# A mixture-of-experts stage with experts ranked by token count, and with fewer slots for the small ones

## What is computed

```python
def swiglu(h, w1, w3, w2):
    return (jax.nn.silu(h @ w1) * (h @ w3)) @ w2

def moe_swiglu(h, router_w, router_b, w1, w3, w2):
    logits = (h @ router_w).astype(jnp.float32) + router_b.astype(jnp.float32)
    top_logit, top_idx = lax.top_k(logits, TOP_K)
    top_p = jax.nn.softmax(top_logit, axis=-1)
    gates = jnp.einsum('btk,btke->bte', top_p,
                       jax.nn.one_hot(top_idx, N_EXPERTS, dtype=jnp.float32)).astype(h.dtype)
    y = jnp.zeros_like(h)
    for e in range(N_EXPERTS):
        y = y + gates[..., e:e + 1] * swiglu(h, w1[e], w3[e], w2[e])
    return y
```

## Time and profile before

| | us |
|---|---|
| median of 3 runs | 3539.58 |
| lowest and highest run | 3536.91, 3546.32 |
| the profiled execution, whole | 3545.75 |
| its span in the profile | 3543.9 |
| the expert work of the eight experts, first matmul to the last | 1724.9 to 2294.2 |
| PE busy over the span | 3007.5 (85%) |

### The profile page before, as it was taken

How to read it: one execution, slowest core, us unless ns; L and a number is a source line. 1 busy time by engine, 2 the same in 40 slices (tenths; PEclk the granted TensorE clock), 3 DMA queues, 4 the chain that set the end, 5 groups by cost and what they waited for, 6 DMA issues and landing times. The chain is left out here.

```text
span 3543.9 us, 59895 instructions
## 1 busy us (share of the span) xinstructions
PE 3007.5 (85%) x26727; PEld 2046.0 (58%) x26727; DVE 1130.1 (32%) x1816; ACT 548.0 (15%) x994; POOL 214.4 (6%) x200
## 2 busy tenths in 40 slices
PE   7998588888787999996799999995797866887875
PEld 2544478888533444443799999984343634544442
DVE  4233578778442010336211111012203723100112
ACT  0001234333201000001100100100201611100001
POOL 1110111111100000000100000001000001000000
PEclk8997699999979999997799999997898987999997
DMA  8522321111405424722477777711211006999994
GB/s 313 182 103 89 85 60 53 53 53 29 162 1 122 136 71 113 268 82 106 166 281 253 254 263 276 259 69 60 97 48 66 1 0 255 425 428 427 426 427 177
DMA packets 242296, 596.96 MB, mean 168 GB/s; under 512 B 25717, under 2 KB 132759, under 8 KB 226553
## 3 DMA queue, kind: packets, MB, share of 16 engines
q1 hardware_dynamic: 210008, 488.85, 37.4%
q0 software_dynamic: 18400, 49.87, 4.9%
q10 hardware_dynamic: 13632, 54.40, 3.9%
HBM read 548.33 MB, written 44.73 MB: 167 GB/s over the span
## 5 line engine op out<-in xcount | busy, mean ns | idle before, releaser
L2712 PE MATMUL ps<-moe_xt,moe_wb 128*128 128x152 f32 (+1 forms) x3168 | 448.8, 303 | 1.7 <-DVE moe_xt L2893 1.1
L2712 PEld LDWEIGHTS ps<-moe_xt,moe_wb 128*128 128x128 f32 x3168 | 435.0, 191 | 11.3 <-issue 1.5
L1653 PE MATMUL ps<-ffn_h,ffn_wb 128*128 128x512 f32 x704 | 304.2, 595 | 17.8 <-PEq L1548 15.5
L2371 PE MATMUL ps<-hier_wb,hier_xt 128*64 128x256 f32 x2048 | 246.1, 396 | 74.0 <-DMA hier_wb<-in_expert_w_up 41.3
L2371 PEld LDWEIGHTS ps<-hier_wb,hier_xt 128*64 128x64 f32 x2048 | 162.5, 143 | 168.8 <-issue 66.8
L1653 PEld LDWEIGHTS ps<-ffn_h,ffn_wb 128*128 128x128 f32 x704 | 134.2, 191 | 187.8 <-issue 187.8
L867 PE MATMUL ps<-AT,X 64*64 64x64 f32 x4608 | 161.4, 227 | 34.2 <-DVE X L1159 30.1
L2719 PE MATMUL ps<-moe_hT,moe_wb 128*128 128x152 f32 x1408 | 187.6, 293 | 0.0
L2719 PEld LDWEIGHTS ps<-moe_hT,moe_wb 128*128 128x128 f32 x1408 | 183.3, 190 | 0.0
L867 PEld LDWEIGHTS ps<-AT,X 64*64 64x64 f32 x4608 | 152.0, 141 | 47.6 <-DVE X L1159 34.9
L1721 PE MATMUL ps<-ffn_g,ffn_wd 128*128 128x512 f32 x352 | 153.0, 598 | 3.0 <-PEq L1616 3.0
(11 more groups left out here) (494 smaller groups left out, 4008.5 us busy)
## 6 DMA issues: line engine op xcount, KB each, us to landing
moe_wb<-in_moe_w SPq DMA_DIRECT2D x54, 2048.0 KB, 10.3
hier_wb<-in_expert_w_gate SPq DMA_DIRECT2D x32, 2048.0 KB, 37.1
hier_wb<-in_expert_w_up SPq DMA_DIRECT2D x32, 2048.0 KB, 38.0
hier_wb<-in_expert_w_down SPq DMA_DIRECT2D x32, 2048.0 KB, 38.4
moe_wb<-in_moe_w SPq DMA_DIRECT2D x27, 1536.0 KB, 8.8
ada_late<-in_ada_w ACTq DMA_DIRECT2D x8, 3072.0 KB, 9.9
ffn_wb<-in_ffn_w SPq DMA_DIRECT2D x22, 1024.0 KB, 7.7
ada_rest<-in_ada_w POOLq DMA_DIRECT2D x64, 256.0 KB, 3.2
```

The lines of the kernel that those rows point to most:

```text
L1653: mm = pe.matmul(k.ps[:, bank + q, :], wb[:, j, q, c, o * P:(o + 1) * P], h[:, c, :], start=c == 0, stop=c == KC - 1)
L2371: mm = pe.matmul(k.ps[both_halves(a), bank, 0:256], xs[:, c, :], wb[:, slot, at:at + 256], start=c == 0, stop=c == KC - 1)
L2712: mm = pe.matmul(k.ps[:, bank, 0:width], wb[:, slot, at:at + P], xs[:, c, :], start=c == 0, stop=c == KC - 1)
```

## The change

The experts of the first stage are ranked on the chip by their token count (ties by number). Rank 0 to 3 keep 152 slots, rank 4 gets 128, ranks 5 to 7 get 64. The blocks run in the order of ranks 0, 5, 1, 6, 2, 7, 3, 4, so the wide blocks stand between narrow ones. Which expert a block's weights come from is now read from `moe_expert_at` into a register of SP.

```diff
-        r = Routing(k, keep, "moe", E, B, BO, OB, 8, 0, False, (64, 43), (T, TO), k.moe_out_d)
+        r = RankedRouting(k, keep, "moe", E, B, BO, OB, 8, 0, False, (64, 51), (T, TO), k.moe_out_d,
+                          narrower=((4, 24), (5, 64)), after_ranks=after_ranks)
...
-            def prefetch(sp):
-                for n in range(RING_M):
-                    load_piece(sp, n)
...
-                stage_layer_norm(k, 1, 0, prefetch=prefetch)
+                stage_layer_norm(k, 1, 0)
...
-                load(sp, n % PIECES, n % RING_M, n // PIECES, landed[n % RING_M])
+                b = n // PIECES
+                if n % PIECES == 0:
+                    rank = ORDER[b]
+                    expert_of[b] = sp.value_load(r.expert_at[0:1, rank:rank + 1], min_val=0, max_val=E - 1)
+                load(sp, n % PIECES, n % RING_M, expert_of[b], landed[n % RING_M])
```

In `route` SP first waits for the ranks, issues the six first pieces, and only then the zeros of `moe_slots`. DVE computes the ranks ahead of the first expert's list, from one more sum of four matmuls:

```diff
             @block.sync
             def _(sp):
+                if ranked:
+                    sp.wait_ge(r.ranked, 1)
+                    r.after_ranks(sp)
                 sp.wait_ge(k.v_for_p.sem, k.v_for_p.at(1))
                 sp.dma_start(slots_d.rearrange("(p b) a -> p (b a)", p=r.zeros[0]), zero[:, :]).then_inc(k.loaded[4].sem, 16)
                 sp.wait_ge(k.loaded[4].sem, k.loaded[4].at(16))
...
+                if ranked:
+                    for q in range(NT):
+                        mm = pe.matmul(k.ps[:, 1, NT * E:(NT + 1) * E], k.square("ones"), both[:, q, :],
+                                       start=q == 0, stop=q == NT - 1)
                 mm.then_inc(k.prod_v.sem, 1)
```

```diff
+                    def few_hidden(n, bank, xs, slot):
+                        width = SLABS[n] * P
+                        weights = wb[:, slot, 0:KC * width].rearrange("p (m a j) -> p m a j", a=2, j=HB)
+                        for c in range(KC):
+                            for a in range(2):
+                                mm = pe.matmul(k.ps[half(a), bank, 0:width // 2], xs[:, c, 0:HB],
+                                               weights[:, c * SLABS[n]:(c + 1) * SLABS[n], a, :],
+                                               start=c == 0, stop=c == KC - 1)
+                        return mm
...
+                    def few_down(f, slot):
+                        for a in range(2):
+                            at = f % 4 * D + a * 512
+                            mm = pe.matmul(k.ps[half(a), 4, :], hT[:, f, 0:HB], wb[:, slot, at:at + 512],
+                                           start=f == 0, stop=f == FC - 1)
+                        return mm
...
+                        hidden(0)
+                        y_before(0)
+                        hidden(1)
+                        y_before(1)
+                        pe.wait_ge(out_taken, b)
+                        turn(0)
+                        hidden(2)
+                        y_before(2)
+                        turn(1)
+                        y_before(3)
+                        products(range(0, 8))
+                        turn(2)
+                        products(range(8, FC))
```

More of the change, by code:

```diff
@@ L1867, in __init__, with slots_of @@
         self.over_token = sb("over_token", [token_rows[1], self.over_blocks * BO // token_rows[1]], I32)
+        self.narrower = ()
+class RankedRouting(Routing):
+    def __init__(self, k, stack, *args, narrower, after_ranks):
+        super().__init__(k, stack, *args)
+        self.narrower, self.after_ranks = narrower, after_ranks
+        self.expert_at = k.sb(f"{self.name}_expert_at", [1, self.E], I32, stack=stack)
+        self.ranked = own_signal(k, stack, f"{self.name}_ranked")
+    def slots_of(self, rank):
+        return self.B - sum(less for first, less in self.narrower if rank >= first)
 def overflow(engine, r, body, left_out=None):
@@ L1958, in route @@
         shift = sb("shift", [P, E], stack=s)
+        ranked = bool(r.narrower)
+        if ranked:
+            key, larger = sb("key", [P, E], stack=s), sb("larger", [P, E, E], stack=s)
+            rank, first = sb("rank", [P, E], stack=s), sb("first", [P, E], stack=s)
+            less, own_slots = sb("less", [P, len(r.narrower), E], stack=s), sb("own_slots", [P, E], stack=s)
+            own, limit = sb("own", [E, E], stack=s), sb("limit", [E, 1], stack=s)
+            place_r, first_place = sb("place_r", [P, NT, E], stack=s), sb("first_place", [P, NT], stack=s)
+            at_rank, expert_f = sb("at_rank", [1, E, E], stack=s), sb("expert_f", [1, E], stack=s)
         with nc.Block() as block:
@@ L2123, in _ @@
                 dve.drain().then_inc(k.v_for_t.sem, 1)
+                if ranked:
+                    for n, (lowest, fewer) in enumerate(r.narrower):
+                        dve.tensor_scalar(less[:, n, :], rank[:, :], float(lowest), float(-fewer), ALU.is_ge, ALU.mult)
+                    dve.tensor_scalar(start0[:, :], rank[:, :], float(B), None, ALU.mult)
+                    dve.drain()
+                    dve.scalar_tensor_tensor(own_slots[:, :], less[:, 0, :], float(B), less[:, 1, :], ALU.add, ALU.add)
+                    dve.drain()
+                    dve.tensor_tensor(own[:, :], own_slots[0:E, :], k.square("ident")[0:E, 0:E], ALU.mult)
+                    dve.drain()
+                    dve.tensor_reduce(limit[:, :], own[:, :], AX.X, ALU.add)
+                    dve.drain()
+                    dve.tensor_tensor(cnt[:, :], cnt[:, :], limit[:, :], ALU.subtract)
+                    dve.drain()
                 dve.tensor_scalar(more[:, :], iota_b[:, :], cnt[:, 0:1], None, ALU.is_lt)
@@ L2545, in stage_first_moe, with counted @@
     ROUNDS = [(0, 3), (3, 6), (6, 8)]
+    SMALL = [rank >= 5 for rank in ORDER]
+    def counted(big, small):
+        return [0, *itertools.accumulate(small if few else big for few in SMALL)]
+    UNITS, X_ROUNDS, Y_ROUNDS = counted(FC, len(SLABS)), counted(len(ROUNDS), 1), counted(4, 0)
+    GATHERS, BIG, FEW = counted(2, 1), counted(1, 0), counted(0, 1)
     w1, w3, w2 = (t[n][0] for n in ("moe_w1", "moe_w3", "moe_w2"))
@@ L2607, in gather_block @@
             def gather_block(pool, b):
-                for a in range(2):
+                rows = HB if SMALL[b] else T
+                for a in range(1 if SMALL[b] else 2):
+                    at = 2 * ORDER[b] + a
                     pool.indirect_dma_start(
-                        out=xg[0:T, a, :], out_offset=None, in_=rows_d,
-                        in_offset=bass.IndirectOffsetOnAxis(ap=r.slot_token[:, 2 * b + a:2 * b + a + 1],
+                        out=xg[0:rows, a, :], out_offset=None, in_=rows_d,
+                        in_offset=bass.IndirectOffsetOnAxis(ap=r.slot_token[0:rows, at:at + 1],
                                                             axis=0)).then_inc(gathered, 16)
@@ L2631, in out_columns, with half, few_bank @@
                 return k.ps[:, 4 + o // 3, o % 3 * B:o % 3 * B + B]
+            def half(a):
+                return slice(HB * a, HB * a + HB)
+            def few_bank(n):
+                return 5 + n % 2
             def over_columns(o):
@@ L2775, in _ @@
+                    for n in range(3):
+                        x_rounds(0, n)
+                    for b in range(E):
+                        pe.wait_ge(xt_ready, X_ROUNDS[b + 1])
+                        (small_block if SMALL[b] else big_block)(b)
                     for n in range(4):
                         y_rounds(E - 1, n)
[L2777 removed]
+                    pe.wait_ge(y_taken, Y_ROUNDS[E])
                     def body(i, odd):
                         b = E + odd
[L2782 removed]
+                        pe.wait_ge(gathered, i * 64 + (16 * GATHERS[E] + 32 * (odd + 1)))
```

285 lines of the change are left out of this document (209 added, 76 removed).

## The result

The changed kernel takes **3487.1 us** (median of 4 runs, 3471.3 to 3488.5), the kernel before beside it 3541.7 (4 runs, 3536.9 to 3546.3). The ratio is 0.9833, with a 95% interval from 0.9818 to 0.9848: 1.7% faster, about 55 us. The forecast was 3448 with a range up to 3474, so the sign was right and the size was not. The profiled execution took 3488.5 us with a span of 3486.7, against a span of 3543.9 before: 57.2 us gained where the sum said 92.2.

What follows compares the result with a forecast made beforehand. The eight expert blocks were taken as bound by PE alone. Blocks 126.3 gained, less 30.6 for the start and 3.5 for the way out, gave 92.2: 3453.6 profiled, median 3448 us, own range 3434 to 3472, whole range 3430 to 3474.

Steps and rivals of the forecast that it cites:

- The fill of zeros: Dense feed-forward stage: 3.2 MB more zeros on idle POOL cost nothing, or 8 us at 410 GB/s without cover.
- The start: Routing to first expert matmul: loads now wait for the ranks, zeros land behind them, gather 30.6 us late (26 to 36).
- Rival B: At the start, the zeros slip past the loads and do not hold the barrier: 26 us less, 3422; 5%.
- The blocks: Eight expert blocks: 443.0 us against 569.3, a gain of 126 us, with 34.5 us for each narrow block.
- C: In narrow blocks, the two halves do not run side by side: 63 us a block, 86 us more, 3534; 4%.
- F: In narrow blocks, loads of the stationary operand are not hidden: at most 32 us in all, 3480; 1%.
- the rule that the prediction cites: Weight loads overlap matmuls only when row groups differ: 15 us more per narrow block, total 45 us later, 3493.
- The ring's estimate: Weight supply to the blocks: stall begins under 332 GB/s, about 1 us slack; no stall taken, bound 5 us at three places.
- Rival D: In the blocks, the weight ring falls behind: 15 to 35 us in all, 3463 to 3483; 3%.
- Rival E: Behind the blocks, one more overflow block runs, costing about 121 us: 3569, slower; 3%.
- The way out: Overflow loop to combine: one more turn with two skipped blocks, 1.2 to 5.9 us, taken as 3.5.
- The scatter ahead of the change: Range term: the runs' own scatter of a few us; no change forecast before the feed-forward stage.

Runs made afterwards that it cites:

- the fill alone: Kernel before, with only the changed kernel's larger zero fill in the feed-forward stage: 3562.3 us against 3544.1, ratio 1.0057.
- paced: Changed kernel with the same zeros written in 14 pieces, each tied to one more finished feed-forward chunk: 3459.3 us, ratio 0.9769.
- z1: Changed kernel with SP issuing the slot table's zeros before the six first weight loads: 3475.7 us, ratio 0.9805.
- z2: Changed kernel with the slot table's zeros first and only three of six weight loads issued in the routing block: 3458.7 us, ratio 0.9754.
- c2: Changed kernel with paced fill, slot-table zeros first, two loads in the routing, the others after the gathered rows land: 3435.5 us, ratio 0.9697.
- o1: Changed kernel with block order 0, 1, 2, 3, 5, 6, 7, 4, the three narrow blocks in a row: 3514.0 us, ratio 0.9906.
- n1: Changed kernel with narrow blocks computed like wide ones, weights stationary and 64 tokens moving: 3557.5 us, ratio 1.0036 to the kernel before.

## Why the prediction was off, point by point

**The fill of zeros is the step that failed.** It reads: "The larger fill of zeros (3.2 MB) lies at the start of the dense feed-forward stage, some 500 us long, on POOL, which has nothing else to do: nothing, and 8 us (3.2 MB at 410 GB/s) if it had no cover." The cover that was named is POOL's. What would have to be free is the 16 engines behind all queues, and at that place PE was already waiting 2.27 us for weights. Its price without cover was wrong too: 3.2 MB at the fill's own 200 GB/s are 16 us, and the runs show 17.9 (the changed kernel: 15.5 more wait and some 2 of lower clock behind it), 17.7 in the trace and 18.2 in the median (the fill alone), and 19.9 gained back (paced). The paced kernel's 3459.3 us lie inside the range that the prediction gave. The figure of 410 GB/s came from the weight loads, another kind of transfer. The Trainium skill's page "DMA: Bandwidth & Descriptors", section "Queues, rings and completion order", says that each DMA engine goes round its queues packet by packet. The trace agrees: from 1165 to 1180, with work in both, it has 720 packets of the fill to 719 of the loads, and at 4 KB to 1 KB a packet the weights got 0.74 of 3.69 MB.

**The start was right in mechanism and 2.7 us short** (33.3 against 30.6). The zeros land behind the loads and the barrier waits for them, as told. What the prediction did not part is that SP's issue of the six loads alone takes 21.7 us: z1 shows 12.4 us of the delay to be the zeros' landing, z2 and c2 that 15 of the remaining 19.5 go with fewer loads to issue. The gather itself was 31.9 us late rather than 30.6, and 1.4 us lie between it and the first matmul. Rival B (the zeros slip past the loads) did not come.

**The blocks gained 120.7, not 126.3.** A narrow block takes 35.7 us, forecast 34.5: the halves run side by side (110 ns for 256 columns, 84 for 192), so rivals C and F fall. With F falls, for this kernel, the rule that the prediction cites from the Trainium skill's page "TensorE: Matmul & The Clock Gate", section "Part 3: Packing small matmuls — row/col tiling", by which its estimate was some 50 us for the block: the trace disagrees with it. The output's turns cost 0.56 us rather than 0.44 between matmuls of the other shape, the next input's turns 1.5 rather than 1.1 in all, and the 44 down records 10.0 us rather than 9.6. ACT's wait was 0.52, forecast 0.53. The first block took 70.7, forecast 72.0: its first 16 us had a granted clock of 0.90, where they had 0.79 before. The other wide blocks took 69.2, 70.1 and 70.5 against 69.1, 69.1 and 69.4, the last two with the short waits for `moe_wb`. Rank 4 took 60.9 against 59.9 (111.7 ns a record, not 110). The ring's estimate (332 GB/s wanted, about 1 us of slack) is as good as the trace: it waited 0.57 and 0.76 us. Rival D came only when the order was changed (o1). Rival E did not come, one overflow block ran.

**The way out was 6.4, not 3.5**, and mostly for other reasons than the one given. From PE's last matmul to the combine it is 4.3 longer: the sum multiplied skips, which are worth about 1.2 us (n1), the low bound, and the rest is a third long branch on PE's queue. The other 2.2 us lie in the overflow block, which is the same in both kernels: PE's part of it took 125.3 us instead of 123.0. The start of its hidden matmuls, before and after (columns as in the earlier trace rows):

```profile
2308.44:2320.00 11.56, 11.56 (x54) 10.19 (x55) 1.27 (x3) 0.77 (x2) 0.00 (x0) 1.00 0.01 1
```

```profile
2243.84:2255.40 11.56, 11.56 (x43) 9.84 (x44) 0.84 (x2) 0.38 (x1) 0.00 (x0) 0.80 0.01 1
```

The clock was lower at its start. In the second execution of the same changed kernel it was 1.00, PE's part took 122.8 us, and the whole way out was 3.4 longer than before: so the forecast's 3.5 was near that by luck, with skips priced too high and a branch and a clock left out.

**The scatter ahead of the change**, 5.1 us in the profiled execution, stands in the range only as "a few us". Without it and without the fill the sum would stand 12 us from the result, within the range.

The rest was 0.9 us. In all: 5.1 + 17.9 + 2.7 + 5.6 + 2.9 + 0.9 = 35 us.

## What to carry to other kernels

Ask of a DMA that grows or moves which transfers share the 16 engines with it and who waits for those, not whether the engine that issues it is idle; a fill that nobody is waiting for should be cut into pieces and tied to the progress of the stage that hides it. A small transfer on whose landing a barrier depends belongs ahead of the large loads on its queue, and the issuing of large loads is itself a wait of the issuing engine. Where a block has 64 tokens, making the tokens stationary is the gain (35.7 us against 61.5), and narrow blocks have to alternate with wide ones for the ring to pay for it.

## What the runs showed of the hardware

- With 128 x 128 stationary operands a record does not get shorter below 128 moving columns: 129.2 ns at 152, 111.7 at 128, 110.8 at 64.
- A fill of DRAM from one broadcast tile moved some 200 GB/s while its queue held 96% of the engines' time (1130 to 1150), half of what the weight loads reach in this kernel. Made 3.2 MB larger, it took the neighbouring loads from 17.1 to 26.5 us. Beside it the engines served one packet of each queue in turn, 720 to 719, of 4 KB and 1 KB.
- An indirect gather beside running loads took 13.0 us to land instead of 5.8.
- A wait of 17.7 us on PE cost some 2 us more behind it, at a granted clock of 0.53.
- Two or three branches on PE's queue over the overflow loop take 3.5 to 6.8 us each, where the others take 0.5 or less. Five 16 KB instruction packets go with two long branches, seven with three; in the one kernel with the same loop and other code ahead of it (n1) there were two.
